# A two-layer hybrid decoder trunk in split float32: the norm's residual formed on GpSimd, products interleaved with the norm's transposes, FFN and w_o in column pairs

## The reference

```python
for l in range(2):
    proj = x @ w_in[l] + b_in[l]                 # queries, keys, values, SSM input, gate logits
    ...                                          # three branches: attention, SSM, memory attention
    merged = g0 * p_sb + g1 * p_ssm + g2 * p_mem
    x = layer_norm(ALPHA * x + merged @ w_o[l], ln1_g[l], ln1_b[l])
    gate, up = split(x @ w_gate_up[l])           # 2048 -> 2 x 5632
    ffn = (silu(gate) * up) @ w_down[l]          # 5632 -> 2048
    x = layer_norm(ALPHA * x + ffn, ln2_g[l], ln2_b[l])
```

## Time and profile before

| | |
|---|---|
| median of 3 runs | 3259.48 us (3258.5 to 3260.88) |
| span of the profiled execution | 3250.4 us |
| the median less that span | 9.1 us |
| PE busy | 3064.7 us, 94% of the span |
| DVE, ACT, POOL busy | 64%, 45%, 6% |
| DMA | 555.62 MB, mean 171 GB/s |
| weight chunk load, from issue to landing | 5.0 to 6.5 us (median, by kind) |

### The profile page before, as it was taken

One profiled execution on the slowest core, in us unless ns is written; L12 is line 12 of the kernel. 1 busy time (PEld: TensorE's weight loads), 2 busy tenths in 40 slices (PEclk: granted clock), 3 DMA queues, 4 the chain that ended last, 5 costly groups with the idle time before them and its releaser, 6 DMA issues.

```text
span 3250.4 us, 49353 instructions
## 1 busy us (share of the span) xinstructions
PE 3064.7 (94%) x16342; PEld 2613.8 (80%) x16342; DVE 2091.9 (64%) x3465; ACT 1467.4 (45%) x2140; POOL 183.2 (6%) x219
## 2 busy tenths in 40 slices
PE   4899899999899999999989998999998999999996
PEld 3777688887788888888877776888877888888885
DVE  4888766665556666656678886666655666566656
ACT  3454455454344444444435554555533444444442
POOL 5100011110000000000000000111100000000002
PEclk8999999999899999999979999999998999999998
DMA  8444467675366666666645454777644666666663
GB/s 238 132 134 134 117 168 200 179 188 193 118 181 182 192 191 186 184 189 192 175 153 144 134 138 123 190 183 196 194 168 117 193 184 191 184 190 181 194 190 120
DMA packets 882169, 555.62 MB, mean 171 GB/s; under 512 B 20568, under 2 KB 817600, under 8 KB 881088
## 3 DMA queue, kind: packets, MB, share of 16 engines
q1 hardware_dynamic: 867536, 541.14, 58.2%
q10 hardware_dynamic: 14576, 13.79, 1.3%
HBM read 546.49 MB, written 8.39 MB: 171 GB/s over the span
## 4 chain that ended last, share of the span: by engine, by line
PE 84%; issue 10%; DVE 2%; POOL 2%; ACTq 1%; ACT 1%; DMA 1%; POOLq 0%; DVEq 0%; SPq 0%
PE bank L1333 38%; PE bank L1334 19%; PE bank L1350 7%; PE bank L1352 7%; PE bank L1351 7%; PE bank L1608 2%; PE bank L1609 1%; PE bank L1407 1%; PE bank L1406 1%; PE bank L1393 1%; PE bank L1457 0%; PE bank L1584 0%; ACTq L651 0%; POOL sp_t L576 0%; DVE rows L1008 0%
## 5 line engine op out<-in xcount | busy, mean ns | idle before, releaser
L1333 PE MATMUL bank<-xs,hi 128*128 128x512 f32 x5376 | 1910.8, 399 | 1.3 <-ACT stage L724 1.3
L1334 PE MATMUL bank<-xs,lo 128*128 128x256 f32 x5376 | 1510.9, 281 | 0.0
L925 DVE TENSOR_TENSOR lo<-raw,hi 128x1024 fp32r<-128x1024 f32 x1016 | 1214.2, 1236 | 233.0 <-ACT hi L610 215.2
L1333 PEld LDWEIGHTS bank<-xs,hi 128*128 128x128 f32 x5376 | 1016.9, 189 | 254.3 <-issue 12.3
L1334 PEld LDWEIGHTS bank<-xs,lo 128*128 128x128 f32 x5376 | 1022.2, 190 | 1.0
L610 ACT ACTIVATE hi<-raw 128x1024 fp32r<-128x1024 f32 x880 | 888.4, 1052 | 255.0 <-PE bank L1352 249.0
L1350 PE MATMUL bank<-hi,mT 128*128 128x512 f32 x960 | 376.4, 392 | 12.7 <-POOL mT L585 12.7
L633 ACT ACTIVATE tmp<-bank 128x256 f32<-128x256 f32 x304 | 111.5, 381 | 602.8 <-PE bank L1334 532.8
L1351 PE MATMUL bank<-lo,mT 128*128 128x512 f32 x960 | 375.3, 391 | 0.0
L1352 PE MATMUL bank<-hi,mT 128*128 128x512 f32 x960 | 375.3, 391 | 0.0
L635 ACT ACTIVATE tmp<-bank,par 128x256 f32<-128x256 f32 x144 | 68.3, 474 | 374.4 <-PE bank L1334 374.4
(11 more groups left out here) (201 smaller groups left out, 2291.1 us busy)
## 6 DMA issues: line engine op xcount, KB each, us to landing
raw<-in_ffn_w_gate_up SPq DMA_DIRECT2D x176, 1024.0 KB, 5.7
raw<-in_w_in SPq DMA_DIRECT2D x160, 1024.0 KB, 6.5
raw<-in_ffn_w_down SPq DMA_DIRECT2D x88, 1024.0 KB, 5.0
raw<-in_w_o SPq DMA_DIRECT2D x32, 1024.0 KB, 5.0
raw<-in_mem_w_kv SPq DMA_DIRECT2D x16, 1024.0 KB, 5.5
raw<-in_sb_w_out SPq DMA_DIRECT2D x32, 512.0 KB, 4.1
raw<-in_ssm_w_out SPq DMA_DIRECT2D x32, 256.0 KB, 4.4
raw<-in_mem_w_out SPq DMA_DIRECT2D x32, 256.0 KB, 4.7
```

What stands on the lines that cost most here:

```text
L925: dve.tensor_tensor(lo[:, s, :], raw[:, slot, h * HALF:(h + 1) * HALF], hi[:, s, :].bitcast(F32), ALU.subtract).then_inc(lo_ready, 1)
L1333: pe.matmul(dst[:, :], hi[:, s, w], x_t[:, k0 + k, :], start=first and k == 0, stop=False)
L1334: ins = pe.matmul(dst[:, 0:T], lo[:, s, w], x_t[:, k0 + k, 0:T], start=False, stop=last and k == 7)
```

## The change

1. **Residual on POOL.** After a norm's centring the rows hold the normalised values. POOL multiplies them by ALPHA·gamma and adds ALPHA·beta in place. Gamma and beta are loaded, broadcast to all partitions, into `gbt` (two DMAs of 1 MB on SP's queue, once in w_o's loads and once before the last FFN turn's), POOL scales it by ALPHA (128x4096), and for every four k-rows, once they are transposed (`ln_T`), makes one multiplication and one addition of 128x2x512. The 64 rebuild matmuls, their copies and semaphores are gone.
2. **First product interleaved.** PE makes the transposes of k = 0 to 3, then for each k the products of the next weights that need only `xs` of that k, then the transposes of k + 4. After w_o these are the first FFN pair (4 matmuls per k), after the FFN the second U chunk (2 per k); the first U chunk, which needs only the memory tokens, runs ahead of the norm. ACT takes over the centring of the rows of the second token tile, and splits a chunk ahead of it.
3. **w_o** reads blocks of 2 k-rows by 1024 columns in k order and waits for each merge on its own; both turns are written out.
4. **FFN in column pairs.** Chunks hold 8 k-rows of 256 columns, gate and up by turns; every eviction step is 512 wide; the down chunks hold 2 k-rows of 1024 columns, and the sums are 1024 wide. `hT` takes the place of `mT`. The very last sums of w_o and of the FFN are made in pieces of 512.

```diff
+            for which in range(2 if l < DEPTH - 1 else 1):
+                v = 2 * l + which
+                pool.wait_ge(gbt_in, 32 * (v + 1))
+                pool.tensor_scalar(gbt[:], gbt[:], ALPHA, None, ALU.mult).then_inc(gbt_scaled, 1)
+                pool.wait_ge(gbt_scaled, v + 1)
+                for c in range(4):
+                    y = rows[:, :, 512 * c:512 * c + 512]
+                    pool.wait_ge(ln_T, 16 * v + 4 * c + 4)
+                    pool.tensor_tensor(y, y, gbt[:, 0:1, 512 * c:512 * c + 512].broadcast_to([P, TT, 512]),
+                                       ALU.mult).then_inc(resid_step, 1)
+                    pool.wait_ge(resid_step, 4 * v + c + 1)
+                    pool.tensor_tensor(y, y, gbt[:, 1:2, 512 * c:512 * c + 512].broadcast_to([P, TT, 512]),
+                                       ALU.add).then_inc(resid_done, 1)
...
 # ACT, norm
+            split_next(ph, l + which, i, c)
+            centre(0)
+            centre(1)
+            for k in range(0, KD, 2):
+                affine(k + 1)
+                if k in (2, 6):
+                    centre(2 + k // 4)
+                hi_part(k)
+                hi_part(k + 1)
...
 # ACT, FFN turn
                     for c in range(12):
-                        if c < 8:
-                            f = c // 2
-                            first_half("FF", l, i, c, bank[2 * (f % 2) + c % 2], done("FF", l, i, c))
...
+                        elif not (first and c == 0):
+                            split_next("FF", l, i, c)
+                        if c < 8 and c % 2:
+                            q, a = c // 2, c // 4
+                            act.wait_ge(half_done, done("FF", l, i, c))
+                            act.wait_ge(tile_out, tile_no("FF", l, i, q) + 1)
+                            act.activation(pt[:, q % 2], banks[:, PAIR_BANK[q]:PAIR_BANK[q] + 2, 0:T], ACT.Copy
+                                           ).then_inc(first_out, 1)
+                            if q % 2 == 0:
+                                act.wait_ge(tile_out, tile_no("FF", l, i, q) + (1 + TILE_CREDIT))
+                                act.activation(th[:], gg[:], ACT.Tanh, scale=0.5).then_inc(ffn_th, 1)
+                            else:
+                                act.wait_ge(ffn_step, n * 4 + (2 * a + 2 + 2))
+                                act.activation(hT[:, 2 * a:2 * a + 2, 0:T], hh[:], ACT.Copy).then_inc(ffn_hi, 1)
...
 # DVE, sums of rows
+            def add_rows(m, n, src, ready, stats=()):
+
+                y = rows[:, m, n:n + 512 * src.shape[1]]
+                dve.wait_ge(*ready)
+                dve.tensor_tensor(y.rearrange("p (a c) -> p a c", c=512), y.rearrange("p (a c) -> p a c", c=512), src,
+                                  ALU.add).then_inc(rows_out, 1)
+                if stats:
+                    dve.wait_ge(rows_out, stats[0] + 1)
+                    for j in range(src.shape[1]):
+                        dve.bn_stats(st[:, m, n // 512 + j, :], y[:, 512 * j:512 * j + 512]).then_inc(stats_done, 1)
...
 # PE, norm
+                for k in range(4):
+                    turn(k)
+                for k in range(KD):
+                    pe.wait_ge(xs_lo, 16 * v + k + 1)
+                    step(k)
+                    if k + 4 < KD:
+                        turn(k + 4)
...
 # PE, w_o
-                pe.wait_ge(merge_lo, 16 * l + 17)
...
+                            for h in range(2):
+                                k = 2 * c + h
+                                if i == 0:
+                                    pe.wait_ge(merge_lo, 16 * l + k + 2)
+                                block_half("WO", l, i, c, h, mT, k, 4 * i, k == 0, k == KD - 1)
```

More of the change, by code:

```diff
@@ L430, in _ @@
[L430 to L436, removed]
+                    return lambda r: [(r.rearrange("p (k n) -> p k n", n=1024), v[:, k0, n0:n0 + 1024])]
@@ L1321, in _ @@
+                ffn_turn(0, True, False)
+                with dve.Fori(1, 10) as i:
+                    ffn_turn(i, False, False)
+                ffn_turn(10, False, True)
                 norm(l, 1)
@@ new lines, in block_terms, with block_half @@
+            def block_terms(src, k, m, s, j, dst, first, last):
+                w = slice(512 * j, 512 * j + 512)
+                xh, xl = src[:, k, m * P:(m + 1) * P], src[:, k, T + m * P:T + (m + 1) * P]
+                pe.matmul(dst, xh, hi[:, s, w], start=first, stop=False)
+                pe.matmul(dst, xh, lo[:, s, w], start=False, stop=False)
+                return pe.matmul(dst, xl, hi[:, s, w], start=False, stop=last)
+            def block_half(ph, l, i, c, h, src, k, base, first, last):
+                s = hl_slot(ph, c, h)
+                pe.wait_ge(lo_ready, chunk_no(ph, l, i, c) * 2 + (h + 1 + HALF_CREDIT))
+                for m in range(TT):
+                    for j in range(2):
+                        ins = block_terms(src, k, m, s, j, bank[base + 2 * m + j], first, last)
+                ins.then_inc(half_done, 1)
@@ L1381, in _, with norm, turn @@
             pe.wait_ge(consts, 2)
-            def norm(l, which):
+            def norm(l, which, step):
                 v = 2 * l + which
-                for k in range(KD):
-                    pe.wait_ge(norm_done, 8 * v + 2 * (k // 4) + 2)
+                def turn(k):
+                    pe.wait_ge(norm_done, 4 * v + k // 4 + 1)
+                    pe.wait_ge(norm_act, 4 * v + k // 4 + 1)
                     if k >= 4:
@@ L1648, in hl_slot, with ffn_turn @@
+                ffn_down(0, False)
+                def ffn_turn(i, last):
+                    for q in range(4):
+                        freed(i, q)
+                        ffn_pair(i, q)
+                    ffn_down(i, last)
+                with pe.Fori(1, 10) as i:
+                    ffn_turn(i, False)
+                ffn_turn(10, True)
 def hl_slot(ph, c, h):
```

389 lines of the change are left out of this document (215 added, 174 removed).

## The result

The changed kernel takes 3269.96 us (median of 12 runs, 3262.54 to 3283.3) against 3258.57 us for the kernel before in 12 runs (3249.41 to 3264.93). The ratio is 1.004, with a 95% interval of 1.0026 to 1.0054: the change makes the kernel slower by 0.4%. The profiled execution spans 3263.2 us, 12.8 more than before.

The account below looks back on a forecast made before the run. PE was taken to bound the kernel (94% busy, alone decisive in the FFN). Terms 17.7 + 26 - 26 - 5.6 - 11 gave 1.1 us gain: span 3249.3, plus 9.1, 3258 us; range 3228 to 3284.

Parts of the forecast that it names:

- C: Rival: POOL and DVE operations exclude each other for their whole length, 8.4 + 5.7 us more, 3272 us; chance 0.29.
- Gain 1, w_o starts at once: At w_o's start in both layers: PE's wait for all merges and the clock dip go, 17.7 us gained.
- Gain 2, the norms: Three norms: old cost 99.6 us beyond useful work, new 73.8, a gain of 26 us.
- a hold of 1.9 us, seven times: In each norm: seven POOL residual operations of 1,024 columns each cost DVE 1.9 us, 13.3 together.
- then DVE is the pace: In each norm after the first xs lo: DVE's lo parts, split halves and affines set the time, 11 us.
- PE's half clock as the lower bound: In a norm: at half clock PE needs 16 x (1.39 + 0.43), 2 us more than DVE; with half-speed tail, gain 16.
- my 34.2 for it: Norm after the FFN: old cost beyond useful work, 32.05 + 4.30/2 = 34.2 us.
- Cost 1, the evictions: FFN: 512-wide eviction steps make PE stand 0.65 and 0.54 us per turn, 26 us lost over 22 turns.
- The wide sums with statistics: First sums of w_o and the last FFN turn, 1,024 wide: 1.4 us late in four places, 5.6 us lost.
- Cost 2, scaling: POOL's scaling of gbt, three times in w_o and the last FFN turn: holds DVE, PE stands about 3 us, 11 us lost.
- At nothing: Counted as free: the weights' new shapes, gamma and beta loads on SP's queue, earlier memT loading; removed rebuild counted in gain 2.
- the 9.1 added at the end: Added to the summed span: the earlier runs' median, 3259.48, lay 9.1 us above the profiled span, 3250.4.

Follow-up runs that it names:

- e1: Changed kernel with POOL's residual operations on 8 columns of each 512, the rest of the residual left out: 3228.44 us, ratio 0.9915 to the kernel before.
- e4: Changed kernel with the residual left out and POOL filling memory with a constant in its place: 3229.41 us, one run.
- e7: Changed kernel with POOL's scaling of gamma and beta in eight 128x512 operations instead of one of 128x4096: 3261.27 us, ratio 0.9995 to the kernel before.
- e5: Kernel before, with w_o's first sum waiting for each merge on its own: 3235.59 us, ratio 0.9941 to the kernel before.
- e2: Changed kernel with POOL scaling only 8 columns of gamma and beta, the rest of the scaling left out: 3257.65 us, ratio 0.9992 to the kernel before.
- e3: Changed kernel with ACT and DVE splitting the next-but-one FFN chunk's first half ahead of an eviction: 3243.39 us, ratio 0.9962 to the kernel before.
- f2: As f1, but DVE forms the residual behind w_o's norms, in the first FFN turn: 3205.56 us, ratio 0.9849 to the kernel before.
- f1: Changed kernel with split before eviction, scaling on ACT in four pieces, POOL's residual after the norm's last transpose in 128x512 pieces: 3220.37 us, ratio 0.9895 to before.

## Why the prediction was wrong

The forecast was 3258 us and "no change", range 3228 to 3284. The time, 3269.96, lies in the range, and the direction doesn't hold: it is slower. Of the rivals it is C whose 3272 came out, and C's mechanism is there, as e1, e4 and e7 show; I gave it 0.29. That its number fits is for the most part luck: of the 14 us that C added to my sum its mechanism gives some 6, and the rest comes from the terms below.

- **Gain 1, w_o starts at once: right.** 17.7 forecast; 13.2 from the waits in the changed kernel, 4.6 from the clock in e5. In the changed kernel the scaling hid the clock's part.
- **Gain 2, the norms: this is the step that failed.** Forecast 26; the two lines with norms show 1.7 and 2.9, with the stops of the FFN's first turns taken off 5.4 together. Two terms stand in it. The term "a hold of 1.9 us, seven times", 13.3 a norm, was about right in its sum: e1 gives 12.6, 16.6 and 13.1 back. The trace has eight held operations of DVE in each norm, 14.7, 13.2 and 14.0 us in all, and their mechanism is C's: a lo that meets a POOL operation of 2.4 to 3.2 us ends with it, up to 2.2 us late. The term that was wrong is "then DVE is the pace". Without POOL the two norms behind w_o gain 13.4 and 14.0 over before, and the third 19.5, where my sum gives 21.4 each and 22.9: 19 us in all, and the rest is POOL's 42 instead of 40. PE at the low clock needed 1.7 us a k-row in the first third (my 1.39 + 0.43), and then the ring through PE, ACT and DVE 1.1, not DVE's 0.7. I had named PE's half clock as the lower bound and then left it out of the sum, with no reason given, and the handovers between the engines stood nowhere in it. In a ring each handover counts. Against a kernel before whose clock rises as in e5 the third norm would gain 10.8 without POOL, and the change would lose 5.8 there; my 34.2 for it rests on the one trace.
- **Cost 1, the evictions: right.** The steps fell where they were forecast, to 0.02 us; the stops are 0.62 and 0.41 instead of 0.65 and 0.54, so 22 turns cost 22.7 us instead of 26. The wide sums with statistics: 0.92 us in w_o and 2.06 in the last turn, two layers, 6.0 against 5.6.
- **Cost 2, scaling: near.** 11 forecast, 14.4 by the stretches of e2. The stops are 2.28 and 1.67 us in w_o and 6.74 in the FFN, where I had 3 for each.
- **At nothing:** the loads of gamma and beta cost nothing (e2 has them), the new chunk shapes neither (e3's turn is that of before). The last stretch, from the last down product to the end, is 2.2 us shorter, which stood nowhere in the sum.
- **Slips in the sum.** The upper bound of gain 2 is called 42; its own figures, 11 for each norm, give 66. The bounds of cost 1 are called 4 to 40; 0.3 for each of 44 places gives 13 to 39. And the 9.1 added at the end is not what lies around a span: every run here is 1.7 to 2.0 us above its own span. The rest is that the traced execution before was some 7 us faster than the median.

Put together, 17.7 + 5.4 - 22.7 - 6.0 - 14.4 makes it 20.0 us slower, which is the sum of the six lines; the 2.2 at the end and the 5.0 in code that the change leaves alone bring it to the 12.8 of the spans. My sum had 1.1 faster, 21.1 us away: 20.6 too much for gain 2, 3.4 too little for the scaling and 0.4 for the wide sums, set off by 3.3 of the evictions. The rule that gave rival C was worth more than the 0.29. The earlier trace rows agreed with it, and so did, which I read as if both operations began together: DVE's began 0.51 us after POOL's and ended 0.55 after its end, so it was held for all that was left of it. But C's 8.4 + 5.7 were the smaller part of what my sum lacked: 2.4 and 3.4 of them came.

## What to carry to other kernels

Before work is given to GpSimd because it is idle, look which VectorE operations with two SBUF inputs stand beside it: each waits for a whole GpSimd operation, so cut GpSimd's to the width that VectorE's slack allows, or keep the work on VectorE: its 11 us cost nothing in the FFN's first turn (f2), while GpSimd's 20 cost 13 beside the norm (e1) and 5 behind it (f1 against f2). Where engines work in a fixed order and a buffer is free before an eviction can start, put the refill ahead of the eviction. And where a loop passes through several engines and back, count its period as the sum of its steps and handovers, not as the busiest engine's work. Before a stretch of one trace is taken as the base, look whether its clock is the same in another trace of the same code.

## What the runs showed of the hardware

- POOL and DVE: a DVE operation with two inputs from SBUF waits for the running POOL operation that reads SBUF. Beside one of 128x4096 (11.02 us) the longest lo took 9.83 us in place of 1.22, and four took 13.24. DVE gets in between two POOL operations even where these stand ready (e7: lo of 1.23 to 1.57 us beside eight POOL operations in 14.28).
- Not held: DVE operations whose tile comes from PSUM (the affine, 0.53 us as alone; in e7 a sum of a bank into `rows`, 1.22 as alone), and xs lo under a POOL fill (0.75 for two, e4).
- Two inputs are not needed for a hold, and a fill is not always free. In the setup of the changed kernel a DVE copy with one input from SBUF, 0.21 us elsewhere, takes 8.93 and ends with a POOL operation; and a DVE operation on 2 columns, at 3.80, takes 1.45 and ends with a POOL fill. Timelines of DVE and POOL for the copy:

```profile
79.42 8.93 DVE L1201 COPY pw<-powers 128x96 f32 x1 [0.35 <-DVE blocks L1128]
```

```profile
77.72 10.57 POOL L572 TENSOR_SCALAR rows<-rows 128x4096 f32<-128x4096 f32 x1
```

- TensorE's clock: the same rebuild matmuls behind the same code ran at a granted clock of 0.50 before and of 1.00 in e5, and the stretch takes 87.3 and 78.6 us.
- POOL's groups in the changed kernel, whose means hold what DVE cost them (xcount | busy us, mean ns):

```profile
L601 POOL TENSOR_SCALAR gbt<-gbt 128x4096 f32<-128x4096 f32 x3 | 32.1, 10706 | 691.7 <-DMA gbt<-in_ln_b 691.7
L609 POOL TENSOR_TENSOR rows<-rows,gbt 128x1024 f32<-128x1024 f32 x12 | 30.7, 2555 | 0.9
L606 POOL TENSOR_TENSOR rows<-rows,gbt 128x1024 f32<-128x1024 f32 x12 | 29.8, 2479 | 252.2 <-PE banks L1489 252.2
```
